# Turning the feed-forward's token-major sums two features at a time

## The reference

```python
    # end of first_block
        u = rms_norm(h, norm_mlp_g[l])
        h = h + jnp.square(jax.nn.relu(u @ w_mlp1[l])) @ w_mlp2[l]   # 1024 -> 4096 -> 1024
    return rms_norm(h, final_norm_g)

    # start of second_block
        h = rmsnorm(x, g_norm[layer])
        proj = h @ w_in[layer]
```

## Time and profile before

| | |
|---|---|
| median of three runs | 1337.95 us (1337.69 to 1338.59) |
| the profiled execution's own time | 1337.92 us |
| its span, first to last instruction | 1336.2 us |
| matmuls (PE) busy | 1322.3 us, 99% |
| weight loads (PEld) busy | 1085.4 us, 81% |
| VectorE (DVE) busy | 1037.7 us, 78% |
| ScalarE (ACT) busy | 625.3 us, 47% |
| mean granted TensorE clock | 0.999 |

### The profile page before, as it was taken

One profiled execution on the slowest core, in us unless ns is written; L12 is line 12 of the kernel. 1 busy time (PEld: TensorE's weight loads), 2 busy tenths in 40 slices (PEclk: granted clock), 3 DMA queues, 4 the chain that ended last, 5 costly groups with the idle time before them and its releaser, 6 DMA issues.

```text
span 1336.2 us, 17173 instructions
## 1 busy us (share of the span) xinstructions
PE 1322.3 (99%) x6369; PEld 1085.4 (81%) x6369; DVE 1037.7 (78%) x1718; ACT 625.3 (47%) x1079; POOL 62.1 (5%) x60
## 2 busy tenths in 40 slices
PE   7999999999999999999999999999999999999998
PEld 6787777788888888888888888888888888888887
DVE  7868888895577877878876565698889988995685
ACT  7435555564455454444334445634333343433234
POOL 1000000102003000000002400000000000000000
PEclk9999999999999999999999999999999999999999
DMA  5333323243324234342333333232233222323332
GB/s 165 95 92 82 74 65 99 64 127 110 107 84 134 78 120 136 101 141 81 123 93 94 101 95 95 84 95 83 79 88 97 84 81 83 104 59 110 102 104 95
DMA packets 204340, 130.33 MB, mean 98 GB/s; under 512 B 21426, under 2 KB 190595, under 8 KB 204258
## 3 DMA queue, kind: packets, MB, share of 16 engines
q1 hardware_dynamic: 202642, 126.62, 32.5%
q10 hardware_dynamic: 1616, 2.62, 0.6%
HBM read 127.12 MB, written 2.10 MB: 97 GB/s over the span
## 4 chain that ended last, share of the span: by engine, by line
PE 95%; DVE 3%; ACT 1%; issue 1%; ACTq 0%; DVEq 0%
PE lin L764 23%; PE lin L768 22%; PE lin L767 22%; PE ob L1299 1%; PE sc L856 1%; PE sc L1162 1%; PE sc L1158 1%; PE sc L1161 1%; PE sc L1255 1%; PE sc L1259 1%; PE tr L1158 1%; PE tr L1162 1%; PE tr L1161 1%; PE sc L1258 1%; PE tr L869 1%; PE ob L893 1%
## 5 line engine op out<-in xcount | busy, mean ns | idle before, releaser
L2050 DVE TENSOR_TENSOR wl<-raw,wh 128x1024 fp32r<-128x1024 f32 (+2 forms) x211 | 251.1, 1192 | 57.3 <-ACT wh L1479 56.4
L1479 ACT ACTIVATE wh<-raw 128x1024 fp32r<-128x1024 f32 (+2 forms) x211 | 214.8, 1020 | 95.9 <-DMA raw<-in_w_mlp_dram 25.7
L764 PE MATMUL lin<-uh,wh 128*128 128x512 f32 x612 | 244.8, 400 | 0.1
L768 PE MATMUL lin<-uh,wl 128*128 128x512 f32 x612 | 238.6, 390 | 0.0
L767 PE MATMUL lin<-ul,wh 128*128 128x512 f32 x612 | 238.4, 390 | 0.0
L764 PE MATMUL lin<-vh,wh 128*128 128x512 f32 x512 | 201.8, 394 | 0.2 <-DVE te L2782 0.2
L768 PE MATMUL lin<-vh,wl 128*128 128x512 f32 x512 | 199.4, 389 | 0.0
L767 PE MATMUL lin<-vl,wh 128*128 128x512 f32 x512 | 199.3, 389 | 0.0
L764 PEld LDWEIGHTS lin<-uh,wh 128*128 128x128 f32 x612 | 114.9, 188 | 26.8 <-issue 3.8
L767 PEld LDWEIGHTS lin<-ul,wh 128*128 128x128 f32 x612 | 115.0, 188 | 24.9 <-issue 2.2
L768 PEld LDWEIGHTS lin<-uh,wl 128*128 128x128 f32 x612 | 114.9, 188 | 24.4
(11 more groups left out here) (688 smaller groups left out, 2515.1 us busy)
## 6 DMA issues: line engine op xcount, KB each, us to landing
raw<-in_w_in_dram SPq DMA_DIRECT2D x100, 512.0 KB, 3.8
raw<-in_w_mlp_dram SPq DMA_DIRECT2D x64, 512.0 KB, 3.9
raw<-in_w_out_dram SPq DMA_DIRECT2D x16, 512.0 KB, 3.5
raw<-in_w_xkv_dram SPq DMA_DIRECT2D x8, 512.0 KB, 3.5
raw<-in_w_proj_b_dram SPq DMA_DIRECT2D x8, 512.0 KB, 3.7
raw<-in_w_proj_a_dram SPq DMA_DIRECT2D x8, 512.0 KB, 3.7
raw<-in_w_mlp_dram SPq DMA_DIRECT2D x12, 256.0 KB, 2.6
xtok<-in_x_dram ACTq DMA_DIRECT2D x4, 512.0 KB, 5.0
```

What stands on the lines that cost most here:

```text
L764: ins = pe.matmul(o, wh[:, slot, at], xh_, start=start, stop=False)
L768: return pe.matmul(o, wl[:, slot, at], xh_, start=False, stop=stop)
L1479: act.activation(wh[:, c.slot(4), 0:size], raw[:, c.slot(2), 0:size], ACT.Copy).then_inc(hi_made, 1)
L2050: dve.tensor_tensor(wl[:, c.slot(4), 0:size], raw[:, c.slot(2), 0:size], wh[:, c.slot(4), 0:size].bitcast(F32), ALU.subtract).then_inc(lo_ ...
```

## The change

TensorE turns tiles 0 and 1 in `up3`'s job 3, tiles 2 and 3 in job 5, tiles 4 and 5 in job 7, each pair ahead of input tile 4, and tiles 6 and 7 ahead of input tile 4 of `down3`'s job 0. Jobs 2, 4 and 6 have no turn. VectorE adds tiles m - 3 and m - 2 after the low part of jobs m = 3, 5 and 7. The waits inside `turn_acc` and `turned_added` are as they were, and so are VectorE's `turned_added(6)` and `turned_added(7)` at the start of `down3`.

```diff
+            def turn_two(f):
+                turn_acc(f)
+                turn_acc(f + 1)
+
             for q in range(4):
                 c, j = phase(f"up{q}")
                 for m in range(DT):
                     if q and m < 2:
                         taken(q - 1, 5 + m)
                     job(c + m, j + m, DT, uh, ul, before=tiles_of(u_low, U0["mlp"]) if q == 0 and m == 0 else None,
-                        between={4: lambda f=m - 2: turn_acc(f)} if q == SEVENS and m > 1 else {})
+                        between={4: lambda f=m - 3: turn_two(f)} if q == SEVENS and m in (3, 5, 7) else {})
...
                 job(c + m, j + m, DT, fh, fl, before=tiles_of(f_low, 12 * SEVENS) if m == 0 else None,
-                    between={2: lambda: turn_acc(DT - 2), 5: lambda: turn_acc(DT - 1)} if m == 0 else {})
+                    between={4: lambda: turn_two(DT - 2)} if m == 0 else {})
...
-                    if q == SEVENS and m > 1:
+                    if q == SEVENS and m in (3, 5, 7):
+                        turned_added(m - 3)
                         turned_added(m - 2)
```

## The result

The changed kernel takes 1340.25 us in the median of 22 runs (1339.87 to 1342.49), the kernel before 1337.99 us (1337.69 to 1339.04, 22 runs). The ratio is 1.0019, 95% interval 1.0013 to 1.0025: 0.19% slower. The profiled execution took 1340.05 us with a span of 1338.3 us, 2.1 us over the span of before. Busy times hardly moved (matmuls 1322.4 us), so the 2.1 us are idle time of TensorE.

The account below looks back on a forecast made before the run. TensorE was taken to bound the kernel, its matmuls filling 99% of the span. Job 0 of `down3` 2.20 us longer, less 0.27 us saved, gave 1337.92 + 1.93 = 1339.85 us, median 1339.9; range with rivals 1338.9 to 1342.2.

Parts of the forecast that it names:

- The last pair waits: In `down3`'s job 0, turns of tiles 6 and 7 stall 1.74 and 1.1 us; job 0 gets 2.20 us longer.
- The pairs in the odd jobs don't wait; VectorE's shift costs nothing: In `up3`'s jobs 3, 5 and 7 turns don't wait (2.8 us to spare in job 5); VectorE's moved additions cost nothing.
- The saving of a pair: Fewer passages between matmuls and transposes save 0.09 us a pair, 0.27 us for three pairs in `up3`.
- The sum of terms: Job 0 of `down3` 2.20 us longer, less 0.27 us saved in `up3`: TensorE 1.93 us late.
- All of the delay reaches the end: After `down3`'s job 0 the 1.93 us pass through in full, with bounds of 1.5 and 2.2 us.
- The rival that part is taken up later: Where VectorE sets the pace later, part of the delay is taken up, leaving 1.2 us: 1339.1 us; chance 0.12.
- The clock: TensorE's clock falls in the stall in `down3`'s job 0, adding 1.4 us: 1341.3 us; chance 0.35.
- The other side: No stall in `down3`'s job 0: the 0.59 us wait goes, four pairs save 0.36: 1337.0 us; chance 0.04.
- The chances: For the whole kernel: slower by over 0.2% 0.40, faster by over 0.2% 0.03, within 0.57; the forecast itself 0.45.

Follow-up runs that it names:

- add_first: The changed kernel with VectorE's pair of additions ahead of the square of jobs 3, 5 and 7 instead of behind their low part: 1337.19 us.
- own_banks: The changed kernel with the turns of tiles 6 and 7 in two other, idle PSUM banks, so they wait for no addition: 1337.11 us.
- after_again: The changed kernel itself, run once more with nothing altered, beside the kernels with added matmuls: 1341.43 us.
- split_4_7: The changed kernel with the last pair split, tile 6 ahead of input tile 4 and tile 7 ahead of input tile 7 of `down3`'s job 0: 1339.23 us.
- filled_pair: The changed kernel with 6 matmuls whose result nothing reads added ahead of the last pair in `down3`'s job 0: 1340.08 us.
- pair_tile7: The changed kernel with the last pair ahead of input tile 7 of `down3`'s job 0 instead of 4: 1338.17 us.
- split_2_5: The changed kernel with tiles 6 and 7 turned ahead of input tiles 2 and 5 of `down3`'s job 0: 1342.13 us.
- pair_tile1: The changed kernel with the last pair ahead of input tile 1 of `down3`'s job 0 instead of 4: 1343.77 us.

## Why the prediction was right

Forecast were 1339.9 us and a range of 1338.9 to 1342.2; measured were 1340.25 us, and 1340.08 in the group with the clock up, 2.1 us over the kernel before where 1.93 were forecast. By its own steps:

- **The last pair waits.** Right in mechanism, place and size. The turns were to come at 715.75 and 717.27 in the times of before, and came at 715.68 and 717.11 with `down3` starting 0.07 us earlier. The second pause was 1.0 us (717.11 - 715.68, less 0.43 of transposes) where 1.1 was forecast, because the turn of tile 7 followed the end of the addition by 0.06 us (717.05) and not by 0.15. Job 0 was to get 2.20 us longer and got 2.16. `add_first` and `own_banks` take away the two links, the order on VectorE and the bank, one at a time, and either removes all of it.
- **The pairs in the odd jobs don't wait; VectorE's shift costs nothing.** Right. VectorE was idle 2.06 us before job 7's square, where it was 1.30 before.
- **The saving of a pair.** Off in size: 0.09 us forecast, 0.04 to 0.05 measured. The forecast took one reading of each and doubled the first. The six single turns of `up3` in the trace of before take 3.42 us four times and 3.44 twice over the same 13 steps, and 3.44 was the reading used; the three pairs of the changed kernel take 3.84, 3.87 and 3.85, and 3.84 was used. The means give 0.05 us a pair. One of each, before and after:

```profile
701.96 0.39 PE L768 MATMUL lin<-uh,wl 128*128 128x512 f32 x1
...
705.38 0.39 PE L764 MATMUL lin<-uh,wh 128*128 128x512 f32 x1
```
```profile
695.56 0.40 PE L768 MATMUL lin<-uh,wl 128*128 128x512 f32 x1
695.79 1.04 PE L1226 MATMUL tr<-ident,acc 128*128 128x128 f32 x8
...
699.43 0.39 PE L764 MATMUL lin<-uh,wh 128*128 128x512 f32 x1
```

  The sum of terms becomes 2.16 - 0.15 = 2.01 us instead of 1.93.
- **All of the delay reaches the end.** Right: 2.0 us at the end of `down3`, 2.1 at the end of the span. The rival that part is taken up later is out.
- **The clock.** A rival with 0.35, and it is about half of the executions: 9 of 22 and 6 of 11. Its price was put at 1.4 us; the medians of the two groups are 1340.08 and 1341.54 us, so 1.5 us, and the two traces differ by 1.30 us in `down3`. Forecast and rival are both true, each of a part of the executions. I had set them against each other as if a kernel were one or the other; a mixture was the right form. That the median came out near the forecast is in part luck: 13 of 22 executions were of the lower group. In the set of `after_again` five of 11 were, and the median was 1341.43 us, 3.3 us over the kernel before instead of 2.3.
- **The other side**, that nothing waits, needed `h_added` = 6 by 713.9; it came at 717.05. `add_first` is that case made real: 1337.2 us, where 1337.0 had been worked out.
- **The chances.** One slip: by the rivals' own chances 0.60 should have lain within 0.2% of before and nothing on a gain of more than that. The 0.57 and 0.03 given there set 0.03 aside for a case that is not in the list.

What stays open: the executions of `split_4_7` (1340.53), `filled_pair` (1341.54) and of the kernel before (four of 33 from 1339.16 to 1339.68 in the first set, one of 27 at 1339.59 in the second) that are slow without a low mean clock. They are too few to bear on any of this.

## What to carry to other kernels

Where two engines hand a double-buffered bank to and fro, grouping the work by two doubles what must be handed back before the next group. Count how far the last member's return lies from the next group's start, above all where the rhythm changes: here the regular distance was two jobs, and one at the seam. First look where the consumer idles; its half of the hand-over can often be put there without touching the producer. And a pause of the matmul engine can cost more than its length: price it with its chance of a lower clock.

## What the runs showed of the hardware

- The changed kernel's pauses of TensorE of 1.7 and 1.0 us, with four transposes between, were followed by the slower time and a mean clock of 0.998 in 15 of 33 executions; in the one of them that was traced the granted clock fell to 0.50. One pause of 1.7 us alone was followed by this in none of 11 (`split_4_7`), one of 0.7 us in none of 11 (`pair_tile7`), one of 3.1 us by the slower time in 9 of 11 (`split_2_5`), and one of 3.8 us with a second behind it in 5 of 5 (`pair_tile1`). The same pause in the same kernel can have it or not.
- The low stretches lasted 3.4 us in `after_again` (716.7 to 720.1) and `split_2_5` (716.4 to 719.8), and about 7 us in `pair_tile1` (714.5 to 721.4), where the pause went on for 1.1 us after the fall. In `after_again` part of it lay in the pause; the last four transposes at twice their distance and some five matmul steps of 0.43 us instead of 0.23 make up the 1.3 us that `down3` took longer.
- Twelve useless matmuls in a pause of 3.1 us made a kernel 1.9 us faster in the median.
- Passing from matmuls to transposes and back costs 0.04 to 0.05 us beyond the transposes themselves, of which four take 0.43 us (713.46 to 713.89 in `add_first`): hardly worth grouping for.
